# Inverse of the delta recurrence: doublings up to 32 on 32x32 tiles of the array, the last one as one 32x32 product per head and chunk

## The reference, cut to what matters

```python
kb = k * beta
lower = jnp.where(strict, jnp.einsum("...id,...jd->...ij", kb, k) * decay, 0.0)
rhs = jnp.concatenate([v * beta, kb * jnp.exp(gc)[..., None]], -1)
sol = lax.linalg.triangular_solve(lower + jnp.eye(chunk, dtype=F32), rhs,
                                  left_side=True, lower=True, unit_diagonal=True)
u, w = sol[..., :dv], sol[..., dv:]
intra = jnp.where(causal, jnp.einsum("...id,...jd->...ij", q, k) * decay, 0.0)
def step(s, inp):                       # one chunk after the other, state s is 64x64 a head
    v_new = u_i - w_i @ s
    o = (q_i * exp(gc_i)) @ s + a_i @ v_new
    s = s * exp(g_last) + (k_i * exp(g_last - gc_i)).T @ v_new
```

## Time and profile before

| | us |
|---|---|
| median of 3 runs | 3611.88 (3608.4 to 3614.02) |
| the profiled execution | 3604.7 |
| its span in the trace | 3603.2 |
| stage_delta in the trace, about | 858 to 1372 |

### The profile page before, as it was taken

One profiled execution on the slowest core, in us unless ns is written; L12 is line 12 of the kernel. 1 busy time (PEld: TensorE's weight loads), 2 busy tenths in 40 slices (PEclk: granted clock), 3 DMA queues, 4 the chain that ended last, 5 costly groups with the idle time before them and its releaser, 6 DMA issues. The chain is left out here.

```text
span 3603.2 us, 67992 instructions
## 1 busy us (share of the span) xinstructions
PE 3350.1 (93%) x27025; PEld 3003.7 (83%) x27025; DVE 2097.7 (58%) x3523; ACT 1473.9 (41%) x2819; POOL 443.6 (12%) x671
## 2 busy tenths in 40 slices
PE   7999999976899996999697799999999999999997
PEld 7899999944788884666586798998999999899995
DVE  2655556654345444666487465665565565575695
ACT  2434444443244443666343343343343343343353
POOL 0000000021456552000133000000000000000000
PEclk8999999987899997999898899999999999999999
DMA  7677766741111115332475644454454454454464
GB/s 225 179 221 225 212 183 185 198 134 39 37 41 41 36 29 179 124 122 85 154 221 186 190 138 152 126 176 149 126 171 151 129 175 147 128 171 141 141 193 131
DMA packets 706406, 521.44 MB, mean 145 GB/s; under 512 B 64648, under 2 KB 650615, under 8 KB 706043
## 3 DMA queue, kind: packets, MB, share of 16 engines
q1 hardware_dynamic: 658312, 427.16, 40.3%
q0 software_dynamic: 26576, 70.12, 5.6%
q10 hardware_dynamic: 21216, 19.93, 1.8%
HBM read 432.11 MB, written 86.05 MB: 144 GB/s over the span
## 5 line engine op out<-in xcount | busy, mean ns | idle before, releaser
L1219 PE MATMUL ps_gate_up<-h2T_group_high,w_gate_up_high 128*128 128x384 f32 (+1 forms) x2112 | 689.5, 326 | 23.7 <-DVE w_gate_up_low L1315 17.4
L1220 PE MATMUL ps_gate_up<-h2T_group_low,w_gate_up_high 128*128 128x384 f32 (+1 forms) x2112 | 688.5, 326 | 0.0
L1221 PE MATMUL ps_gate_up<-h2T_group_high,w_gate_up_low 128*128 128x384 f32 (+1 forms) x2112 | 688.4, 326 | 0.0
L1219 PEld LDWEIGHTS ps_gate_up<-h2T_group_high,w_gate_up_high 128*128 128x128 f32 x2112 | 398.7, 189 | 26.4 <-issue 26.4
L1220 PEld LDWEIGHTS ps_gate_up<-h2T_group_low,w_gate_up_high 128*128 128x128 f32 x2112 | 398.8, 189 | 0.0
L1221 PEld LDWEIGHTS ps_gate_up<-h2T_group_high,w_gate_up_low 128*128 128x128 f32 x2112 | 398.7, 189 | 0.0
L1315 DVE TENSOR_TENSOR w_gate_up_low<-w_gate_up,w_gate_up_high 128x1024 fp32r<-128x1024 f32 x264 | 322.3, 1222 | 63.1 <-ACT w_gate_up_high L1253 51.6
L1321 DVE TENSOR_TENSOR w_down_low<-w_down_ring,w_down_high 128x512 fp32r<-128x512 f32 x264 | 182.4, 693 | 290.9 <-ACT w_down_high L1259 290.7
L1253 ACT ACTIVATE w_gate_up_high<-w_gate_up 128x1024 fp32r<-128x1024 f32 x264 | 279.1, 1057 | 162.0 <-PE ps_gate_up L1221 136.8
L1259 ACT ACTIVATE w_down_high<-w_down_ring 128x512 fp32r<-128x512 f32 x264 | 166.0, 631 | 331.7 <-PE ps_down L1231 166.0
L433 PE MATMUL ps_feature<-hT_high,w_in_high 128*128 128x384 f32 (+1 forms) x816 | 271.6, 333 | 9.8 <-DVE hT_low L607 8.4
(11 more groups left out here) (445 smaller groups left out, 6647.9 us busy)
## 6 DMA issues: line engine op xcount, KB each, us to landing
w_gate_up<-in_w_gate SPq DMA_DIRECT2D x132, 512.0 KB, 3.7
w_gate_up<-in_w_up SPq DMA_DIRECT2D x132, 512.0 KB, 3.8
w_down_ring<-in_w_down SPq DMA_DIRECT2D x264, 256.0 KB, 2.6
w_in_ring<-in_w_in SPq DMA_DIRECT2D x84, 512.0 KB, 4.2
w_ada_ring<-in_w_ada SPq DMA_DIRECT2D x48, 512.0 KB, 5.2
s_ck_rows<-in_cache_c_k SPq DMA_DIRECT2D x32, 512.0 KB, 6.8
s_cv_rows<-in_cache_c_v SPq DMA_DIRECT2D x32, 512.0 KB, 5.0
d_convT<-scratch_convT SPq DMA_DIRECT2D x17, 576.0 KB, 4.3
```

The lines of the kernel that those rows point to most:

```text
L1219: pe.matmul(out, w_high, h_high, start=(k == 0), stop=False)
L1220: pe.matmul(out, w_high, h_low, start=False, stop=False)
L1221: last = pe.matmul(out, w_low, h_high, start=False, stop=(k == DC - 1))
```

## The change

Three helpers stand beside `quadrants`. `within_blocks` computes one product as 24 matmuls of 32x32 by 32x32: for each head the four diagonal blocks of 32 rows (partitions 0, 32, 64, 96), which are four different 32x32 tiles on the diagonal of the array. It is used for all products of levels 1 to 4. At level 5, Y is only the lower left 32x32 block of each 64x64 block (`across_blocks`, 12 matmuls), and only the upper right block of the transposed inverse is added to (`across_turned`, 12 matmuls). `first_inverse` stays on `quadrants`. What the copies, masks and waits do is as before; the copies still move all 384 columns. `ps_Y` is zeroed once at the start of the stage, as its parts outside the diagonal blocks are copied but not written at levels 1 to 4.

```diff
@@ -2635,6 +2635,30 @@
+            def within_blocks(bank, lhs, rhs, first):
+                for i in range(H):
+                    for b in range(4):
+                        r, o = slice(b * 32, b * 32 + 32), b % 2 * 32
+                        last = pe.matmul(bank[r, i * C + o:i * C + o + 32], lhs(r, i, o), rhs(r, i, o), start=first and i == 0,
+                                         stop=True, skip_group_check=True)
+                return last
+
+            def across_blocks(bank, lhs, rhs):
+                for i in range(H):
+                    for c in range(2):
+                        top, bottom = slice(c * C, c * C + 32), slice(c * C + 32, c * C + C)
+                        last = pe.matmul(bank[bottom, i * C:i * C + 32], lhs(top, i, 32), rhs(top, i, 0), start=i == 0,
+                                         stop=True, skip_group_check=True)
+                return last
+
+            def across_turned(bank, lhs, rhs):
+                for i in range(H):
+                    for c in range(2):
+                        top, bottom = slice(c * C, c * C + 32), slice(c * C + 32, c * C + C)
+                        last = pe.matmul(bank[top, i * C + 32:i * C + C], lhs(bottom, i, 0), rhs(bottom, i, 32), start=False,
+                                         stop=True, skip_group_check=True)
+                return last
@@ -2707,7 +2731,11 @@
-                quadrants(ps_Y, lambda r, i: L[r, l, i, :], lambda r, i: X[r, i, :], True).then_inc(s["Y_done"], 1)
+                lower, inverse = lambda r, i, o: L[r, l, i, o:o + 32], lambda r, i, o: X[r, i, o:o + 32]
+                if l < 5:
+                    within_blocks(ps_Y, lower, inverse, True).then_inc(s["Y_done"], 1)
+                else:
+                    across_blocks(ps_Y, lower, inverse).then_inc(s["Y_done"], 1)
@@ -2717,9 +2745,13 @@
+                product, turned_inverse = lambda r, i, o: Y[r, i, o:o + 32], lambda r, i, o: turned[r, i, o:o + 32]
                 if l < last_level(n):
-                    quadrants(ps_X[:, 0], lambda r, i: turned[r, i, :], lambda r, i: Y[r, i, :], False).then_inc(s["Z_done0"], 1)
-                quadrants(ps_X[:, 1], lambda r, i: Y[r, i, :], lambda r, i: turned[r, i, :], False).then_inc(s["Z_done1"], 1)
+                    within_blocks(ps_X[:, 0], turned_inverse, product, False).then_inc(s["Z_done0"], 1)
+                if l < 5:
+                    within_blocks(ps_X[:, 1], product, turned_inverse, False).then_inc(s["Z_done1"], 1)
+                else:
+                    across_turned(ps_X[:, 1], product, turned_inverse).then_inc(s["Z_done1"], 1)
@@ -3055,6 +3087,7 @@
         @block.vector
         def _(dve):
+            dve.memset(ps_Y[:, 0:W], 0.0)
```

## The result

The changed kernel takes 3639.27 us (median of 4 runs, 3635.01 to 3644.57) against 3610.43 us for the kernel before, measured beside it (4 runs, 3608.40 to 3614.02). The ratio is 1.0078, 95% interval 1.0062 to 1.0093: slower by 29 us, where 38 us less was forecast.

What follows compares the result with a forecast made beforehand. It took POOL and a tied DVE chain to bound A, PE mostly B. Saving 2.27 us in 14 rounds gave 32, plus 2 (round 1), 3.5 (tile 16), 0.5 (tile 0): 38 off 3611.9, forecast 3574 us, range 3556 to 3616.

Steps and rivals of the forecast that it cites:

- The product, 0.70 to 0.38 us: Each level 1 to 4 product: 48 pairs, four tiles at once, 8 ns a pair, saving 0.32 us.
- Rival 1: 32-column pairs cost their tile as before, or tiles don't overlap: 3613 us (chance 0.17) or 3602 us (0.12).
- B: Rest of a round, LX2 to next `matrices(k+1, 1)`, 16.8 us, PE-bound but for two places: saves 2.27 us.
- the one before LX3, at 0.10: New tile-size change between `intra` and LX3 in level 3, leaving 0.86 us of 0.96; bounds 0 and 0.2.
- forecast 0.96, 0.96 and 0.45: Savings a round in levels 2, 3 (before its tile-size change) and 4, the last limited by ACT's weights.
- A: End of `matrices(k+1, 1)` to LX2, 9.40 us, set by POOL and a DVE chain: shorter products gain 0.
- Rival 3: PE idles more in A, so its clock falls to 1.2 GHz half the time: 3700 us and more; chance 0.03.
- Rival 2: PE's sequencer delivers pairs no faster than 26 ns, so a product takes 1.25 us: 3696 us; chance 0.13.

Runs made afterwards that it cites:

- levels234: The changed kernel with only levels 2, 3 and 4 on 32x32 tiles, levels 1 and 5 on 64x64 as before; 13 us slower than the kernel before.
- level3: The kernel before with only level 3 on 32x32 tiles, all else on 64x64; 0.27% faster than the kernel before.
- level4: The kernel before with only level 4 on 32x32 tiles, all else on 64x64; 0 us against the kernel before.
- levels15: The changed kernel with only levels 1 and 5 on 32x32 tiles, levels 2 to 4 on 64x64; 21 us slower than the kernel before.
- level5: The kernel before with only level 5's two products on 32x32 tiles, the rest on 64x64; 3633.7 us, 28 us slower than the kernel before.
- level5fill: level5 plus six bf16 128x128x128 matmuls, unread, behind LX5 and six behind Z1 of level 5 each round; 3622.9 us.

## Why the prediction was wrong, step by step

- **The product, 0.70 to 0.38 us:** right. 8 to 9 ns a pair, four tiles at once, 0.62 us by the trace's count where 0.58 was named. Rival 1 falls: 64 columns on the same tiles take 15 ns a pair, 32 take 8 to 9. With it falls, for this kernel, the overhead of about 60 cycles that the Trainium skill's "TensorEngine Tiling (Array Packing)" (Instruction Overhead) puts on every matmul, and that small ones should not be tiled because of it: by it both widths should have cost the same. The floor of about 25 ns from start to start in the Trainium skill's "TensorE: Matmul & The Clock Gate" (Wait — 56ns, not 53.3ns?) isn't seen either between starts on four tiles in bursts (8 to 9 ns); on the average each of the four gets a pair only every 34 ns, which lies above that floor. The 28 ns a pair of the instruction packets is close to it, but is worked out from packets and not from the tiles' starts.
- **B saves 2.27 us:** nearly right where nothing disturbs. The shortest parts of the change sum to 14.76 us, of levels234 likewise, against 16.72: 1.96 saved. The difference is the new changes of tile size, of which I charged only the one before LX3, at 0.10: level3 shows LX2 to LX3 0.20 longer (`intra` to LX3), level4 LX3 to LX4 0.31 longer (`products` to LX4). Without these seams the three levels give 0.87, 0.92 and 0.69 (forecast 0.96, 0.96 and 0.45), 2.48 in all; less 0.51 it is the 1.97 found. What the change really had in B is 16.26 us, 0.52 saved, for pauses and the half clock at its end took the rest.
- **A stays at 9.40, "nothing is gained":** the step that failed. I asked only whether shorter products could make A shorter, and priced the answer at 0, with 0.7 as the worst. Thinning PE's work in that stretch had a price: A is 12.04 us in the mean, 2.48 longer than before, at the low clock for most of it. The same two products of level 5 alone give 11.98.
- **Rival 3, "unlikely", 0.03:** it was the main cause, in a milder form than I had priced, some 9 us of each round at the low level (143 in fifteen rounds) and not half of it. I looked for idle gaps of PE, and the stretch has none at the low clock. With hindsight the timeline had a warning: some of the round's thinnest matmuls stand in A (L2668 moves two columns), and LX5 and Z1 of level 5 were among its few dense products.
- **Rival 2, 0.13:** its pace was right (26 ns a pair; the packets give 28), its sum wrong. Short runs pass without a pause, so the price is no 0.55 us a product but a pause of mostly 0.5 to 2 us where short products crowd, 24 us in all instead of 84.

How the 29 us divide is only partly settled. Over twelve rounds A lost 12 x 2.48 = 30 us and B won 12 x 0.52 = 6; level 5 alone loses 29 (12 x 2.42) in A. In levels15, with the same level 5, A lost only 1.12 a round and the kernel less than level5 did. Why level 1 on 32x32 spares it some of the falls stays open. (The prediction's chances add up to 0.67 for faster and 0.16 for slower, where it writes 0.66 and 0.17; nothing hangs on it.)

## What to carry to other kernels

Ask of a smaller matmul not only what it saves but what the array then does: on a path that another engine bounds, a shorter product brings nothing, and here it brought the clock down to half for microseconds behind it, with PE shown as busy throughout. Count instructions as well as columns: halving the work of each and doubling their number paid here only in short runs with longer matmuls between them. So change the few products on the PE-bound path, one at a time, and leave the others as they are: here three or four products of fourteen gave the most of all kernels tried (3596 and 3594 against 3606 us), and the rest took it away.

## What the runs showed of the hardware that I had not expected

- PE can be granted 1.2 GHz while its busy share is 100% (level5, 1083 to 1093: a mean of 0.57, at the low level from 1084.4 on), and 2.4 GHz at 97% in the same stretch with twelve full-array bf16 matmuls added (level5fill: 1.00).
- Four 32x32 tiles of one array do work beside each other: 48 pairs start within 0.40 us at 2.4 GHz, and take 0.80 us to the next group at 1.2 GHz.
- Instruction packets of 16 KB never started closer than 3.2 us in these rounds, and pauses of 0.4 to 2.2 us for "issue" inside a product end 1.2 to 1.6 us behind the end of one.
- A change of tile size costs 0.20 us between 64x64 and 32x32 (level3), and 0.31 from 64-row matmuls of 128 columns to 32x32 (level4).
